# The out projection of a decoder layer: chunks 0 and 1 as a pair of seven half products, chunk 2 spread between them

## The chip, the core and the metric

The kernel runs on one core of a Trainium2 chip. The metric is the device time in microseconds (us), as the median of several runs; the trace beside it is one profiled execution. The engines are TensorE (PE: matmuls, with PEld for the weight loads ahead of them), VectorE (DVE), ScalarE (ACT), GpSimd (POOL) and SyncE (SP, which here only issues transfers). Each works through its own list of instructions in order; semaphores hold one engine until another has come to a point. A DMA can be issued by SP, ACT or POOL.

## The reference

One decoder layer on 256 positions of 2048 features, in float32. What matters here is its middle: the merged branches are multiplied by `w_out` and added to `x`, and the result goes to the FFN.

```
SEQ, D_MODEL, D_FF = 256, 2048, 5632
h = rms_norm(x, g_attn[l])
proj = h @ w_in[l]                       # queries, keys, values, forget gates, ga, gb
...
merged = sigmoid(ga) * (o_a @ w_br_fox[l]) + sigmoid(gb) * (o_b @ w_br_dil[l])
x = x + merged @ w_out[l]                # the out projection: 256 x 2048 by 2048 x 2048
h = rms_norm(x, g_ffn[l])
u = h @ w_up[l]                          # 2048 x 11264, then a causal convolution, SwiGLU
...
x = x + (silu(gate) * val) @ w_down[l]
```

## The kernel before

**Products and units.** A float32 product is made of three: each operand is split into a high part (what TensorE's fp32r type keeps) and a low part (the rest), and w_hi·a_h + w_lo·a_h + w_hi·a_l is summed in PSUM. The work is a list of *units*, one weight tile of 256 x 512 each (512 KB). A whole unit makes 12 matmuls of 128x512: 2 blocks of 128 rows x 2 slices of 128 features x 3 (`rows_unit`). The time of the kernel is that of TensorE's list of units, from unit 0 to the last.

**The way of a weight tile.** A DMA brings it into a buffer: `raw` has 4 slots (RAW_SLOTS), `raw_x` and `raw_y` have two each. Then ACT writes its high part into `w_hi` (`high(n)`, L1259), DVE subtracts and writes the low part into `w_lo` (`low(n)`, L1776), and TensorE reads both. `w_hi` and `w_lo` have 6 slots (RING): beside unit n, ACT and DVE make the parts of unit n+6, and `high` waits until unit n has been used. Three semaphores count units: `hi_done`, `lo_done`, `used`. SP reloads a `raw` slot when the low part of the unit that held it is done.

**Products of a pair.** The gates and the FFN, but in the kernel before not the out projection, have a second form. Two chunks of 512 columns are taken together, a matrix of 2 x 2 blocks on the features and columns, and half of the features go through seven products, P1 to P7, instead of eight (Strassen's scheme in Winograd's form). Such a product covers one block of 128 rows, as two half units q = 0, 1 of 6 matmuls each; the other features go through plain units. Its operands are sums: of the activations (`make_sums` and the parts P3, P5, P6, P7, made by DVE, split by ACT and DVE: `part_high`, `part_low`) and of the weight tiles. The sums of weights are made in place in `raw_x` and `raw_y`: by an *adding transfer* (POOL issues a DMA that adds the tile from memory to what the buffer holds), or by a sum on DVE (L1785, in `low`). Within a pair the order is P3, P1, P7, P6, P5, P2, P4. P1's tile is in raw_x, P3's in raw_y; P7 and P6 are in raw_y, P5 and P2 in raw_x, P4 in raw_y. P3's and P5's sums of weights come by adding transfer, P7's by DVE; for P6's follower P4 (the *fourth product* of raw_y) `low` has DVE add raw_x to raw_y at P2. The products land in PSUM banks that also collect plain units; copies on ACT (negated or not) and sums on DVE carry products from bank to bank.

**The branch stage**, ahead of the out projection, has 32 units in four chunks (BR_UNIT). After each chunk DVE adds the branch's banks to `work` (`dil_part`, L2120), then the two branches to `tmp` (L2124); TensorE turns `tmp` by transposes, ACT copies the high parts into `actA` (L1285, `merged_high`), DVE the low parts (L1828, `merged_low`). A chunk of `merged` is done once per branch chunk; the last one (chunk 3) in the out projection.

**The out projection** (OUT_UNIT, 24 units) has chunks 0, 1 and 2 of 512 columns, 8 units each, in this order. OUT_BANKS gives two banks to each, one per block of rows. At the end of a chunk `add_x2` on DVE adds both banks to `xr`, the copy of `x` in `work` (L2156), which ACT had loaded again with one DMA of 2 MB at unit 1 (x_again); TensorE then turns the sum (`turn_x2`), ACT copies it (`x2t_copy`) and sums its squares (`x2_squares`). Chunk 3 stands in block 0 of the FFN, as "O" units between its first products. Behind unit 3 of chunk 2 DVE makes the FFN's sums (`make_sums`, L1904 to L1909); ACT splits them at units 4 and 5, DVE at units 5 and 6. The loads of the FFN's first products are behind the last load of the out projection on SP's queue.

What sets the order around the change is written out by hand: each engine has its own loop over the same list of units, and what it does beside a unit is tied to the unit's place.

```
RING = 6
QU = 2
PAIRS = 7
OUT_BANKS = ((6, 7), (1, 3), (0, 2))
```

PAIRS is the number of pairs in the gates; the index PAIRS (the eighth) is free there.

## Time and profile before

| | us |
|---|---|
| median of 3 runs | 1336.09 (1335.77 to 1336.88) |
| the profiled execution | 1335.9 |
| its span, first to last instruction | 1333.9 |
| TensorE busy in it | 1329.0 |
| DVE busy | 1121.8 |
| ACT busy | 941.5 |
| out projection on TensorE, 552.90 to the FFN's first product at 621.04 | 68.1 |

The profiled execution takes 2.0 us more than its span, for what lies around the first and the last instruction. The page gives the busy time of each engine over the span, the chain of work that ended last, and the costliest groups of instructions. A row of the timeline has the start, the duration, the engine, the line, the operation and its tiles, and in brackets the idle time ahead of it with what ended that. Matmuls overlap: the duration of one is longer than the distance to the next, and only the distance adds up.

### The profile page before, as it was taken

What the parts mean: (1) busy time and instruction counts of PE and PEld (TensorE: products, weight loads), DVE (VectorE), ACT (ScalarE), POOL (GpSimd) and SP (SyncE); (2) the same over time, 40 slices, a digit from 0 to 9 for tenths busy, and PEclk for the clock granted to TensorE, in tenths of its full rate; (3) what the DMA queues carried; (4) which work ended last, traced back from release to release, by engine and by line L of the source; (5) the groups of instructions that cost most, each with busy time, mean ns of one, the idle gap of its engine ahead of it and who ended that gap; (6) DMA issues with size and microseconds to landing.
All of it is one profiled execution on the core that took longest, in us unless ns stands there. A gap on an engine that the chain in (4) does not pass through costs nothing.

```text
span 1333.9 us, 16454 instructions
## 1 busy us (share of the span) xinstructions
PE 1329.0 (100%) x6055; PEld 1101.7 (83%) x6055; DVE 1121.8 (84%) x1334; ACT 941.5 (71%) x1181; POOL 156.4 (12%) x175
## 2 busy tenths in 40 slices
PE   9999999999999999999999999999999999999999
PEld 7888888888888888888888888888888888888887
DVE  6868787888888876657688898999999999999996
ACT  6666666666666654446777778888888888888872
POOL 0121212021011000001010101111111102020200
PEclk9999999999999999999999999999999999999999
DMA  9877685758888654667879688999989899999952
GB/s 357 285 176 255 143 268 115 246 145 239 229 219 227 206 177 171 213 228 224 273 171 335 159 301 171 314 219 283 245 254 268 229 288 213 302 209 311 202 192 106
DMA packets 118191, 305.73 MB, mean 229 GB/s; under 512 B 11864, under 2 KB 13152, under 8 KB 117600
## 3 DMA queue, kind: packets, MB, share of 16 engines
q1 hardware_dynamic: 92304, 234.57, 50.5%
q0 software_dynamic: 21728, 66.07, 27.8%
q10 hardware_dynamic: 4080, 4.05, 0.9%
q8 instruction: 48, 0.79, 0.3%
q14 instruction: 31, 0.25, 0.1%
HBM read 302.55 MB, written 2.11 MB: 228 GB/s over the span
## 4 chain that ended last, share of the span: by engine, by line
PE 98%; DMA 1%; DVE 0%; ACT 0%; issue 0%; SPq 0%; ACTq 0%
PE acc L746 13%; PE acc L750 13%; PE acc L748 13%; PE acc L786 9%; PE acc L790 9%; PE acc L788 9%; PE acc L973 4%; PE acc L977 4%; PE acc L975 4%; PE acc L948 3%; PE acc L950 3%; PE acc L952 3%; PE acc L1085 1%; PE acc L769 1%; PE acc L767 1%; PE acc L771 1%
## 5 line engine op out<-in xcount | busy, mean ns | idle before, releaser
L1776 DVE TENSOR_TENSOR w_lo<-raw,w_hi 128x1024 fp32r<-128x1024 f32 x233 | 282.6, 1220 | 89.2 <-ACT w_hi L1259 87.9
L1259 ACT ACTIVATE w_hi<-raw 128x1024 fp32r<-128x1024 f32 x233 | 243.7, 1054 | 110.2 <-PE acc L750 76.6
L746 PE MATMUL acc<-w_hi,actA 128*128 128x512 f32 x660 | 259.7, 394 | 0.1
L750 PE MATMUL acc<-w_hi,actA 128*128 128x512 f32 x660 | 257.3, 390 | 0.0
L748 PE MATMUL acc<-w_lo,actA 128*128 128x512 f32 x660 | 256.9, 389 | 0.0
L1259 ACT ACTIVATE w_hi<-raw_y 128x1024 fp32r<-128x1024 f32 x144 | 149.8, 1058 | 75.4 <-PE acc L750 22.6
L1776 DVE TENSOR_TENSOR w_lo<-raw_y,w_hi 128x1024 fp32r<-128x1024 f32 x144 | 173.2, 1219 | 23.4 <-ACT w_hi L1259 22.1
L1776 DVE TENSOR_TENSOR w_lo<-raw_x,w_hi 128x1024 fp32r<-128x1024 f32 x108 | 129.9, 1219 | 40.5 <-ACT w_hi L1259 40.1
L750 PEld LDWEIGHTS acc<-w_hi,actA 128*128 128x128 f32 x660 | 123.9, 188 | 26.1
L746 PEld LDWEIGHTS acc<-w_hi,actA 128*128 128x128 f32 x660 | 123.9, 188 | 25.5 <-issue 0.7
L748 PEld LDWEIGHTS acc<-w_lo,actA 128*128 128x128 f32 x660 | 124.0, 188 | 24.9
L1259 ACT ACTIVATE w_hi<-raw_x 128x1024 fp32r<-128x1024 f32 x108 | 111.1, 1051 | 36.4 <-DMA raw_x<-w_in 19.3
L786 PE MATMUL acc<-w_hi,actB 128*128 128x512 f32 x296 | 116.3, 393 | 0.0
L790 PE MATMUL acc<-w_hi,actB 128*128 128x512 f32 x296 | 115.4, 390 | 0.0
L788 PE MATMUL acc<-w_lo,actB 128*128 128x512 f32 x296 | 115.1, 389 | 0.0
L973 PE MATMUL acc<-w_hi,actA 128*128 128x512 f32 x224 | 88.3, 394 | 0.0
L977 PE MATMUL acc<-w_hi,actA 128*128 128x512 f32 x224 | 87.3, 390 | 0.0
L975 PE MATMUL acc<-w_lo,actA 128*128 128x512 f32 x224 | 87.2, 389 | 0.0
L2422 POOL DMA_DIRECT2D raw_y<-w_up x34 | 29.5, 868 | 459.1 <-DVE w_lo L1776 458.9
L1259 ACT ACTIVATE w_hi<-odd 128x1024 fp32r<-128x1024 f32 x63 | 66.3, 1053 | 17.3 <-PE acc L790 9.9
L1776 DVE TENSOR_TENSOR w_lo<-odd,w_hi 128x1024 fp32r<-128x1024 f32 x63 | 76.7, 1217 | 1.8 <-ACT w_hi L1259 1.8
L2195 DVE SCALAR_TENSOR_TENSOR work<-acc,smalls_sb,work 128x255 f32<-128x255 f32 (+1 forms) x176 | 72.4, 473 | 3.4 <-ACT work L1595 3.3
(300 smaller groups left out, 2606.9 us busy)
## 6 DMA issues: line engine op xcount, KB each, us to landing
raw<-w_in SPq DMA_DIRECT2D x101, 512.0 KB, 4.7
raw<-w_down SPq DMA_DIRECT2D x59, 512.0 KB, 5.6
raw_x<-w_up SPq DMA_DIRECT2D x44, 512.0 KB, 5.0
raw_y<-w_up POOLq DMA_DIRECT2D x34, 512.0 KB, 7.4
raw_x<-w_in SPq DMA_DIRECT2D x28, 512.0 KB, 4.0
raw<-w_out SPq DMA_DIRECT2D x28, 512.0 KB, 4.6
odd<-w_up SPq DMA_DIRECT2D x27, 512.0 KB, 5.1
work<-w_up SPq DMA_DIRECT2D x24, 512.0 KB, 5.5
```

The costliest lines, as they stand in the source:

```text
L746: nc.tensor.matmul(o, lhsT=a_h, rhs=w_hi[:, s, k, :], start=first and k == 0, stop=False, skip_group_check=onto_seed)
L748: nc.tensor.matmul(o, lhsT=a_h, rhs=w_lo[:, s, k, :], start=False, stop=False, skip_group_check=onto_seed)
L750: mm = nc.tensor.matmul(o, lhsT=a_l, rhs=w_hi[:, s, k, :], start=False, stop=last and k == KU - 1, skip_group_check=onto_seed)
L786: nc.tensor.matmul(o, lhsT=a_h, rhs=w_hi[:, s, k, :], start=first and k == 0, stop=False, skip_group_check=True)
L788: nc.tensor.matmul(o, lhsT=a_h, rhs=w_lo[:, s, k, :], start=False, stop=False, skip_group_check=True)
L790: mm = nc.tensor.matmul(o, lhsT=a_l, rhs=w_hi[:, s, k, :], start=False, stop=last and k == KU - 1, skip_group_check=True)
L973: nc.tensor.matmul(o, lhsT=a_h, rhs=w_hi[:, s, k, :], start=side == 0 and j == 0 and k == 0, stop=False, skip_group_check=True)
L975: nc.tensor.matmul(o, lhsT=a_h, rhs=w_lo[:, s, k, :], start=False, stop=False, skip_group_check=True)
L977: mm = nc.tensor.matmul(o, lhsT=a_l, rhs=w_hi[:, s, k, :], start=False, stop=kt == KT - 1, skip_group_check=True)
L1259: nc.scalar.activation(w_hi[:, n % RING, :, :], src.rearrange("p (k n) -> p k n", k=KU), ACT.Copy).then_inc(hi_done, 1)
L1776: nc.vector.tensor_tensor(w_lo[:, n % RING, :, :], src.rearrange("p (k n) -> p k n", k=KU), w_hi[:, n % RING, :, :].bitcast(f32), ALU.subt ...
L2195: t = nc.vector.scalar_tensor_tensor(out=conv[:, j, lag:SEQ], in0=bank[(4, 7)[j // 2]][:, (j % 2) * SEQ:(j % 2 + 1) * SEQ - lag], scalar=s ...
```

## The change

**What it does.** Chunks 0 and 1 of the out projection become a pair (index PAIRS, 7, in the tables of the gates). Its first eight slices of features go through the seven products on half of the rows' blocks, 14 half units "H"; the other eight through plain units "G" (side 0 and 1, plain 0 to 3), 8 of them. Chunk 2's eight units "C" are spread: `out_units` writes the order C0, P3, C1, P1, C2, P7, P6, G00, P5, G01, G10, P2, G02, P4, G03, G11, G12, G13, C3 to C7, 30 units (each P is two half units; G01 is side 0 plain 1).

**Banks and sums.** OUT_BANKS now names a bank for each product; chunk 2 has banks 6 and 7. ACT copies P1 (negated) from bank 0 to bank 1, P7 from bank 3 to `tmp`, P6 (negated) from bank 0 to `tmp` (`out_sum`). DVE adds bank 0 to `xr` (g_u0) ahead of the second row block of G10, subtracts P7 and adds P6 (`out_bank_sums`). TensorE waits for g_v7 ahead of G00's second row block and for g_u0 ahead of G10's. `add_x2` is left for chunk 2 alone.

**Operands.** ACT makes a second, whole copy of the turned `merged` in `odd` (`merged_turned`); DVE subtracts there (`make_merged`, at the end of the branch stage), ACT and DVE split the results (`merged_part_high`, `merged_part_low`). ACT makes P1's negated parts with two copies.

**Loads.** 24 tiles become 28: SP loads 22, and POOL issues six adding transfers, two each for P3, P5 (as in the gates) and for P4. P4's are the second point of the change: instead of the sum on DVE at P2, the adding transfer is issued when P6's low part is done. The reload of `x` is split in two DMAs of 1 MB, at P1's first half and at P5's first half. The FFN's first loads follow P2 and P4.

**Moved.** The transposes of chunk 3 of `merged` go behind C1 (they were behind unit 2 of chunk 0), those of chunk 0 of the new x behind G12, of chunk 1 behind C3. `make_sums` goes from behind unit 3 of chunk 2 to behind unit 4, the copies P3 and P1 of `part_high` from 4 to 5, P7 and P6 from 5 to 6, `part_low` from 5 and 6 to 6 and 7. The FFN's first O unit waits for `x2_done` 3.

The core of the diff (line numbers behind @@ are of before and after):

```diff
@@ -50,18 +50,18 @@
 def uses_before(i, q):
-    return (PAIRS if q < QU else 0) + i - first_block(q)
+    return (PAIRS + 1 if q < QU else 0) + i - first_block(q)
...
@@ -108,7 +108,29 @@
-FF_UNIT = OUT_UNIT + 3 * UPR
+def out_units():
...
+    units = third(0) + product("P3") + third(1) + product("P1") + third(2) + product("P7") + product("P6")
+    units += plain(0, 0) + product("P5") + plain(0, 1) + plain(1, 0) + product("P2") + plain(0, 2)
+    return units + product("P4") + plain(0, 3) + plain(1, 1, 2, 3) + third(*range(3, UPR))
...
@@ -161,7 +196,7 @@
-OUT_BANKS = ((6, 7), (1, 3), (0, 2))
+OUT_BANKS = {"P3": 2, "P1": 0, "P7": 3, "P6": 0, "P5": 0, "P2": 1, "P4": 3}
@@ -671,16 +719,43 @@ SP
...
+            for n, unit in enumerate(OUTS, OUT_UNIT):
+                if unit[0] != "H":
+                    k = OUT_LOAD_AT[unit] + RAW_SLOTS
+                    if k < len(OUT_LOADS):
+                        sp.wait_ge(lo_done, n)
+                        load_out(k)
+                    continue
+                _, c, name, q = unit
+                if name == "P5":
+                    sp.wait_ge(lo_done, n)
+                    load_gate_b21(c, q)
+                elif name == "P2":
+                    sp.wait_ge(lo_done, n)
+                    load_b11(0, q)
...
@@ -1059,23 +1134,77 @@ TensorE
+            def out_product(n, name, q):
+                if q == 0:
+                    if name == "P3":
+                        pe.wait_ge(dil_merged, 4)
+                        pe.wait_ge(h_part_lo, 5)
+                    elif name == "P1":
+                        pe.wait_ge(h_part_hi, 9)
+                    elif name == "P7":
+                        pe.wait_ge(h_part_lo, 6)
+                    elif name == "P6":
+                        pe.wait_ge(h_part_lo, 7)
+                        pe.wait_ge(g_p1, PAIRS + 1)
+                    elif name == "P5":
+                        pe.wait_ge(h_part_lo, 8)
+                        pe.wait_ge(g_v, PAIRS + 1)
+                o = bank[OUT_BANKS[name]]
+                pe.wait_ge(lo_done, n)
...
+            def out_plain(n, side, j):
+                pe.wait_ge(mt_lo, 6 if j < 2 else 8)
+                pe.wait_ge(lo_done, n)
+                s = n % RING
+                for r, o in enumerate((bank[2], bank[0]) if side else (bank[1], bank[3])):
+                    if r and j == 0:
+                        pe.wait_ge(g_u0 if side else g_v7, PAIRS + 1)
...
@@ -1186,6 +1315,8 @@
                 if unit[0] == "O":
                     u = unit[2]
+                    if u == 0:
+                        pe.wait_ge(x2_done, 3)
@@ -1564,24 +1704,59 @@ ACT
+                    elif c == 3 and u == 1:
+                        act.wait_ge(mt_lo, 2)
+                        merged_part_high("P3", 12)
+                        for half in range(2):
+                            nc.scalar.activation(own[:, 0, :, half * P:half * P + P],
+                                                 gate_quarter(0, 0, half).bitcast(f32), ACT.Copy, scale=-1.0)\
+                                .then_inc(h_part_hi, 1)
...
+            def out_sum(n, name):
+                act.wait_ge(used, n + 1)
+                if name == "P1":
+                    act.wait_ge(dil_merged, 3)
+                    nc.scalar.activation(bank[1], bank[0], ACT.Copy, scale=-1.0).then_inc(g_p1, 1)
+                elif name == "P7":
+                    nc.scalar.activation(tmp[:, 1, :], bank[3], ACT.Copy).then_inc(g_v7, 1)
+                else:
+                    nc.scalar.activation(tmp[:, 0, :], bank[0], ACT.Copy, scale=-1.0).then_inc(g_v, 1)
...
+                elif unit == ("H", PAIRS, "P1", 0):
+                    act.dma_start(xr[:, :, 0:2 * NB], x_rows[:, :, 0:2 * NB]).then_inc(x_again, 16)
+                elif unit == ("H", PAIRS, "P5", 0):
+                    act.wait_ge(x_again, 16)
+                    act.dma_start(xr[:, :, 2 * NB:], x_rows[:, :, 2 * NB:]).then_inc(x_again, 16)
...
@@ -1775,12 +1951,12 @@ DVE, in low
-                if (GATE_UNIT <= n < BR_UNIT and GATES[n - GATE_UNIT][2] == "P2"
+                if (pair and name == "P2" and c < PAIRS
                         or n >= FF_UNIT and FFN[n - FF_UNIT][2] == "P2" and not fourth_by_transfer(i, q)):
...
@@ -2138,6 +2314,23 @@ DVE
+            def make_merged():
+                x11, x21, x12, x22 = (merged_sum[name] for name in ("P6", "P7", "P3", "P5"))
+                nc.vector.tensor_tensor(x22, x21, x22, ALU.subtract).then_inc(h_made, 1)
...
+            def merged_part_low(name, n_hi):
+                dve.wait_ge(h_part_hi, n_hi)
...
+                    elif c == 3 and u == 0:
+                        make_merged()
+                    elif c == 3 and u == 2:
+                        merged_part_low("P3", 7)
@@ -2156,23 +2353,59 @@
+            def out_bank_sums(n, unit):
+                if unit == ("H", PAIRS, "P5", QU - 1):
+                    dve.wait_ge(x_again, 16)
+                    dve.wait_ge(used, n + 1)
+                    add_bank(0, out_rows(0, 1)).then_inc(g_u0, 1)
+                elif unit == ("G", PAIRS, 0, 1):
+                    dve.wait_ge(g_v7, PAIRS + 1)
...
+                elif unit == ("C", 4):
+                    make_sums()
+                elif unit == ("C", 6):
+                    part_low("P3")
+                    part_low("P1")
...
@@ -2417,6 +2650,15 @@ POOL
+            third_sum(PAIRS, 0)
+            third_sum(PAIRS, 1)
+            first_sum(PAIRS, 0)
+            first_sum(PAIRS, 1)
+            for q in range(QU):
+                pool.wait_ge(lo_done, OUT_AT["H", PAIRS, "P6", q])
+                nc.gpsimd.dma_start(raw_y[:, q, :].rearrange("p (k n) -> p k n", k=KU),
+                                    w_out_v[:, KU * (QU + q):KU * (QU + q) + KU, 0:NB], accum_op=ALU.add)\
+                    .then_inc(y_summed[q], 16)
```

**Where instructions stand.** The three pieces below list DVE's and POOL's instructions in their order, before and after; the lines of after are its own (L1952 is `low`, L1776 before; L2360 `add_bank`; L2616 and L2659 adding transfers).

DVE from the low parts behind the last `merged_low` to chunk 1's sums, before (L2156 is `add_x2`):

```order
L1776 TENSOR_TENSOR w_lo<-raw,w_hi 128x1024 [waits hi_done] x5
L1828 TENSOR_TENSOR actA<-acc,actA 128x2x256 [waits mt_hi] x2
L1776 TENSOR_TENSOR w_lo<-raw,w_hi 128x1024 [waits hi_done] x3
L2156 TENSOR_TENSOR work<-acc,work 128x512 [waits unit_used,x_again]
L2156 TENSOR_TENSOR work<-acc,work 128x512
L1776 TENSOR_TENSOR w_lo<-raw,w_hi 128x1024 [waits hi_done] x8
L2156 TENSOR_TENSOR work<-acc,work 128x512 [waits unit_used]
L2156 TENSOR_TENSOR work<-acc,work 128x512
```

The same place after:

```order
L1952 TENSOR_TENSOR w_lo<-raw,w_hi 128x1024 [waits hi_done]
L1952 TENSOR_TENSOR w_lo<-raw_x,w_hi 128x1024 [waits hi_done] x2
L1952 TENSOR_TENSOR w_lo<-raw,w_hi 128x1024 [waits hi_done] x2
L1952 TENSOR_TENSOR w_lo<-raw_x,w_hi 128x1024 [waits hi_done] x2
L1952 TENSOR_TENSOR w_lo<-raw,w_hi 128x1024 [waits hi_done]
L2360 TENSOR_TENSOR work<-acc,work 128x512 [waits unit_used,x_again]
L1952 TENSOR_TENSOR w_lo<-raw_y,w_hi 128x1024 [waits hi_done]
L2370 TENSOR_TENSOR work<-work,tmp 128x512 [waits g_v7]
L1952 TENSOR_TENSOR w_lo<-raw_y,w_hi 128x1024 [waits hi_done]
L2374 TENSOR_TENSOR work<-work,tmp 128x512 [waits g_v]
```

The sum of bank 0 (L2360, g_u0) now stands behind the low parts of P2's two tiles (the second raw_x x2) and of G02 (raw), and the sums with P7 (L2370) and P6 (L2374) among P4's tiles; no sum of raw_y and raw_x stands at P2.

DVE at the end of the out projection, before (L1904 to L1909 `make_sums`, L1847 and L1844 low halves of FFN operands):

```order
L1776 TENSOR_TENSOR w_lo<-raw,w_hi 128x1024 [waits hi_done] x3
L1776 TENSOR_TENSOR w_lo<-raw_y,w_hi 128x1024 [waits hi_done] x2
L1904 TENSOR_TENSOR odd<-work 128x512 [waits x2t_done]
L1906 TENSOR_TENSOR odd<-work,odd 128x512 [waits part_made]
L1907 TENSOR_TENSOR odd<-work 128x512
L1909 TENSOR_TENSOR odd<-work,odd 128x512 [waits part_made]
L1776 TENSOR_TENSOR w_lo<-softmax,w_hi 128x1024 [waits hi_done]
L1776 TENSOR_TENSOR w_lo<-raw_x,w_hi 128x1024 [waits hi_done]
L1847 TENSOR_TENSOR actB<-odd,actB 128x4x128 [waits part_hi]
L1844 SCALAR_TENSOR_TENSOR actB<-work,actB 128x4x128 [waits part_hi]
L1776 TENSOR_TENSOR w_lo<-raw_x,w_hi 128x1024 [waits hi_done]
```

The same place after (L2080 to L2085 `make_sums`, L2023 and L2020 the low halves):

```order
L1952 TENSOR_TENSOR w_lo<-raw_y,w_hi 128x1024 [waits hi_done] x2
L1952 TENSOR_TENSOR w_lo<-softmax,w_hi 128x1024 [waits hi_done]
L2080 TENSOR_TENSOR odd<-work 128x512 [waits x2t_done]
L2082 TENSOR_TENSOR odd<-work,odd 128x512 [waits part_made]
L2083 TENSOR_TENSOR odd<-work 128x512
L2085 TENSOR_TENSOR odd<-work,odd 128x512 [waits part_made]
L1952 TENSOR_TENSOR w_lo<-raw_x,w_hi 128x1024 [waits hi_done] x2
L2023 TENSOR_TENSOR actB<-odd,actB 128x4x128 [waits part_hi]
L2020 SCALAR_TENSOR_TENSOR actB<-work,actB 128x4x128 [waits part_hi]
```

`make_sums` stands one tile later, behind the softmax buffer's tile (third of block 0's tiles made there) and not ahead of it, and the low halves behind both raw_x tiles and not between them.

POOL's adding transfers from the branch stage's end to the FFN's first, before:

```order
L2357 COPY st<-smalls_sb 128x1 [waits row_max]
L2359 TENSOR_TENSOR softmax<-consts_sb,st 128x384 [waits slope_now]
L2422 DMA raw_y<-w_up 128x1024 [waits lo_done] x2
L2422 DMA raw_x<-w_up 128x1024 [waits y_added0]
L2422 DMA raw_x<-w_up 128x1024 [waits y_added1]
L2422 DMA raw_y<-w_up 128x1024 [waits lo_done] x2
```

and after (w_out rows are new):

```order
L2590 COPY st<-smalls_sb 128x1 [waits row_max]
L2592 TENSOR_TENSOR softmax<-consts_sb,st 128x384 [waits slope_now]
L2616 DMA raw_y<-w_out 128x2x512 [waits lo_done] x2
L2616 DMA raw_x<-w_out 128x2x512 [waits y_added0]
L2616 DMA raw_x<-w_out 128x2x512 [waits y_added1]
L2659 DMA raw_y<-w_out 128x2x512 [waits lo_done] x2
L2664 DMA raw_y<-w_up 128x1024 [waits lo_done] x2
L2664 DMA raw_x<-w_up 128x1024 [waits y_added0]
L2664 DMA raw_x<-w_up 128x1024 [waits y_added1]
L2664 DMA raw_y<-w_up 128x1024 [waits lo_done] x2
```

The pair's six adding transfers stand ahead of the FFN's, the fourth product's two (L2659) last of the six.

## Rows read from the trace of the kernel before

**Rows 1.** Page, busy time; and windows: us, PE, PEld, DVE, ACT, POOL, PEclk, DMA, GB/s.

```profile
PE 1329.0 (100%) x6055; PEld 1101.7 (83%) x6055; DVE 1121.8 (84%) x1334; ACT 941.5 (71%) x1181; POOL 156.4 (12%) x175
...
552.00:618.00 66.00, 65.89 (x303) 54.49 (x302) 36.70 (x38) 32.46 (x45) 1.76 (x2) 1.00 0.76 257
```

**Rows 2.** Waits of TensorE: us in total, times, longest us.

```profile
PE acc L873 <- POOL actB L2371: 1.3, 1, 1.3
```

**Rows 3.** Timeline of TensorE at both ends of the out projection.

```profile
552.40 0.39 PE L750 MATMUL acc<-w_hi,actB 128*128 128x512 f32 x1
552.90 0.47 PE L746 MATMUL acc<-w_hi,actA 128*128 128x512 f32 x1
...
618.32 0.39 PE L746 MATMUL acc<-w_hi,actA 128*128 128x512 f32 x1
...
621.04 0.39 PE L786 MATMUL acc<-w_hi,actB 128*128 128x512 f32 x1
```

**Rows 4.** Timelines of DVE, then ACT, at the branch stage's end.

```profile
543.59 2.56 DVE L1776 TENSOR_TENSOR w_lo<-raw,w_hi 128x1024 fp32r<-128x1024 f32 x2
...
551.51 1.28 DVE L1828 TENSOR_TENSOR actA<-acc,actA 128x512 fp32r<-128x512 f32 x2
552.90 1.29 DVE L2120 TENSOR_TENSOR work<-acc,work 128x512 f32<-128x512 f32 x2
...
546.55 1.06 ACT L1259 ACTIVATE w_hi<-raw 128x1024 fp32r<-128x1024 f32 x1 [1.66 <-PE acc L750]
549.28 1.06 ACT L1259 ACTIVATE w_hi<-raw 128x1024 fp32r<-128x1024 f32 x1 [1.67 <-PE acc L750]
```

**Rows 5.** Timelines of ACT, then DVE, at the out projection's end.

```profile
610.42 1.06 ACT L1259 ACTIVATE w_hi<-raw_y 128x1024 fp32r<-128x1024 f32 x1 [1.12 <-PE acc L750]
...
615.43 0.64 ACT L1319 ACTIVATE actB<-odd 128x512 fp32r<-128x512 f32 x1 [1.23 <-DVE odd L1909]
615.97 0.62 ACT L1319 ACTIVATE actB<-work 128x512 fp32r<-128x512 f32 x1
...
611.51 1.23 DVE L1776 TENSOR_TENSOR w_lo<-raw_y,w_hi 128x1024 fp32r<-128x1024 f32 x1 [2.41 <-ACT w_hi L1259]
612.66 0.68 DVE L1904 TENSOR_TENSOR odd<-work 128x512 f32<-128x512 f32 x1
...
618.71 0.68 DVE L1847 TENSOR_TENSOR actB<-odd,actB 128x512 fp32r<-128x512 f32 x1
```

**Rows 6.** Last gate pair: timelines of POOL, ACT, SP's queue and TensorE.

```profile
424.98 1.20 POOL L2383 DMA_DIRECT2D raw_x<-w_in  x1 [2.30 <-DVE raw_y L1785]
...
430.66 1.06 ACT L1259 ACTIVATE w_hi<-raw_x 128x1024 fp32r<-128x1024 f32 x1 [0.71 <-DMA raw_x<-w_in]
...
436.86 1.06 ACT L1259 ACTIVATE w_hi<-raw_x 128x1024 fp32r<-128x1024 f32 x1 [0.18 <-DMA raw_x<-w_in]
...
429.68 3.70 SPq L588 DMA_DIRECT2D raw_x<-w_in  x2
...
442.37 0.39 PE L948 MATMUL acc<-w_hi,actA 128*128 128x512 f32 x1
```

**Rows 7.** Transfers issued in 556 to 574: KB each, median us to landing.

```profile
raw<-w_out SPq DMA_DIRECT2D x7, 512.0 KB, 6.3
work<-x ACTq DMA_DIRECT2D x1, 2048.0 KB, 11.3
```

**Rows 8.** Transfers issued in 571 to 594.

```profile
raw<-w_out SPq DMA_DIRECT2D x9, 512.0 KB, 4.2
```

**Rows 9.** Transfers issued in 628 to 652, block 0 of the FFN.

```profile
raw_y<-w_up POOLq DMA_DIRECT2D x2, 512.0 KB, 10.4
raw_x<-w_up SPq DMA_DIRECT2D x2, 512.0 KB, 8.6
```

**Rows 10.** Timeline of TensorE at the kernel's start.

```profile
1.32 4.21 PE L873 MATMUL acc<-actB 128*128 128x512 f32 x9 [1.32 <-POOL actB L2371]
5.32 0.54 PE L844 MATMUL acc<-w_hi,actA 128*128 128x512 f32 x1
```

261 lines of the change are left out of this document (190 added, 71 removed).

## The prediction

> **What bounds the kernel now.** Four views, in this order. The page's busy times first: TensorE is busy for 1329.0 of 1333.9 us [rows 1], so a product taken away counts in full unless something makes TensorE wait. Then its waits: the one of any size is the 1.3 us ahead of the first instruction [rows 2]. The out projection has the granted clock 1.00 (2.4 GHz) over the whole stretch [rows 1]. Then TensorE's timeline: a product of 128x512 starts every 0.227 us (the 0.39 us of a row is latency), so a unit of 12 takes 2.72 us, 618.32 to 621.04 [rows 3], and one of 6 products 1.36 us. Last, what the other engines have in hand over TensorE, because each weight tile passes load, ACT's high part and DVE's low part, in order on each engine: a late tile also holds whatever stands behind it on ACT and DVE. So the question is not how much work is removed, but which of these queues comes late.
>
> **Removed: 12 products.** Chunks 0 and 1 were 16 units of 12, 192 products. Now they are 14 half units of 6 (84) and 8 plain units of 12 (96), 180 together. 12 x 0.227 = 2.72 us, on the path in full. The three transposes of the stage stay, moved.
>
> **The first product, P3.** Before, the stage starts 0.50 us after the last branch product, 552.40 to 552.90, a wait of 0.27, for DVE's merged halves (551.51 + 1.28) [rows 3, 4]. Now chunk 2's first unit (C0) needs only older halves: it starts at 552.63 and ends at 555.35. P3 then waits for two things that the change itself makes late: its operand, and bank 2, which the last dil_part empties. DVE's two lows end at 546.15 [rows 4]; the four new subtractions take 2.75 us (the same four in block 0: 612.66 to about 615.4 [rows 5]), to 548.9. ACT, free at 547.6 after the tile of 546.55, waits for that and then makes three part copies, 0.54 apart, to 550.6; the tile that started at 549.28 is 1.3 us late, and so are the merged halves behind it. DVE adds P3's low half (0.6) ahead of them: halves 553.4 to 554.7, dil_part (1.29) to 556.0. P3 waits 0.65 us; less the 0.27 that goes: **+0.4 us** (0 if ACT's copies are quicker, 0.8 with one more late step).
>
> **The end of the stage.** In before the chain to block 0's P3 is: tile 610.42, low 611.51, four sums from 612.66, part copies on ACT from 615.43, another tile, its low, P3's low half 618.71 to 619.4 [rows 5]. P3 starts at 621.04 [rows 3], 1.65 us later. The change puts make_sums behind C4, the copies behind C5 and the low half behind C6, each one unit nearer to the end. 2.72 - 1.65 = **+1.1 us** (0.8 to 1.3). Nothing covers it: the same operations in the same order, all of them with rows. Block 0's unit O0 now waits for chunk 2's sums: DVE 0.1 + 1.29 after the stage, against 2.72 of P3's two halves, so nothing.
>
> **The transfers in the middle.** With P3 at 556.0, TensorE without waits goes on with P3, C1, eight transposes, P1 and C2: 4 x 2.72 + 0.95 (552.90 to 621.04 less 24 x 2.72 leaves 2.9 us for three such sets [rows 3]), P7 at 567.8. P7 and P6 lead to side 0 plain 0 at 573.3 (its second row block 1.36 later, 574.6), P5 at 576.0, and side 1 plain 0 at 581.4 (second row block at 582.8). Both second blocks have a new wait.
> First g_v7, an ACT copy of bank 3. DVE, behind dil_part, has the merged add (1.23), three lows (1.14 apart), a part (0.6) and P7's first sum (1.23): 556.0 + 6.5 = 562.5, and a low and a sum later, at 564.9, the second; GpSimd issues the adding transfers for P5 there. In the last gate pair such a transfer issued at 424.98 was in at 430.66, where ACT waited for it: 5.7 us [rows 6]. Here the second has 2.4 us after the first, and half of x (1 MB) starts on ACT's queue at about 565.9. While the whole x flowed, loads of w_out took 6.3 us in the median against 4.2 alone, and x itself 11.3 [rows 7, 8]. I take 9 us for the second transfer, 574; ACT's tile (1.0) and the copy (0.6) end at 575.6. **+1.0 us** (0 with 5.7, 2 with 10).
> Then g_u0. It is a sum on DVE, and ahead of it DVE has the lows of both P2 tiles and of side 0 plain 2. P2's tiles are loaded by SP into the buffers that P5 has just left, so they are issued after P5's lows: 571.5 and about 576.3 (574 + 1.06 + 1.14). GpSimd's queue then still has the two adding transfers of the fourth product (the new part; one DVE sum each, 1.23 us, goes). Between adding transfers in block 0, SP's raw_x loads took 8.6 us and GpSimd's 10.4 in the median [rows 9]; in the gate pair, with the queue empty by then, P2's second tile was read at 436.86 after SP's issue at 433.0 (the row of two issues ends at 433.38), some 3.9 us [rows 6]. With 3.9 the second tile is in at 580.2, and tile, two lows and the sum (1.06 + 1.14 + 1.14 + 0.7, some 4.1 us) end at 584.3, against 583.8 needed after the first wait: +0.5. With 8.6: 584.9, 589.0, +5.2. The nearer row is the one with 8.6, since adding transfers and SP's loads are under way together as there, though with fewer loads: I take 7.7, **+4.3 us**. For the range, 0 (if x and the sums come no later than in the gate pair) to 5.2.
> After that P2's lows are done, and the fourth product's transfers have 20 us.
> The Trainium skill, DMA: Bandwidth & Descriptors, section Issuing engines are not separate DMA queues, says that DMAs started by different engines run on the same 16 DMA engines and interleave. The trace agrees (6.3 against 4.2 us). With queues of their own the +1.0 and +4.3 would be gone, and the sum would be the first rival's.
>
> **Edits that cost nothing.** ACT gets 6 part copies, 4 copies of turned halves, 3 bank copies and 6 more tiles, about 15 us over 75; it is busy 32.5 of 66 us there [rows 1]. DVE gets 6 lows, 8 sums and parts, 2 P7 sums and 3 bank sums, some 17 us on 36.7 of 66 [rows 1]. Room is left in sum; the order costs, and that stands above. If this cover were gone, each further low would be 1.2 us. The loads for the first four tiles are issued in the branch stage, 20 us ahead. Loads grow from 24 tiles to 28, half a megabyte each.
>
> **Sum.** -2.72 + 0.4 + 1.1 + 1.0 + 4.3 = +4.1 us on the profiled execution's 1335.9 (span 1333.9 and 2.0 around it): 1340.0. The median of the runs is 0.2 above that execution; I say 1340.2.
>
> **Rivals.**
> 1. The transfers land in time, not slower: x in two halves of 4 KB rows disturbs less than 2 MB at once, and the gate pair runs the same pattern with no wait on TensorE. For it: there P2's first half started at 442.37, five us after its second tile was read at 436.86 [rows 6]. Against it: no x and no fourth transfer there, and no sum of DVE behind those lows. It decides at P2's second tile: in by 578.7 (4.1 ahead of 582.8), no wait. Sum -2.72 + 0.4 + 1.1 = -1.2: 1334.9.
> 2. The low halves are in time too, at both ends, and nothing waits: -2.72 - 0.27 = -3.0, 1333.1. Against it are the durations of rows 4 and 5, that do not depend on transfers.
> 3. It gets worse at the same place: the second P5 transfer takes 11 us as x did, so everything behind it moves 2 us on, and TensorE stands for 6 to 7 us there. If the clock falls in such a wait, that costs more: the nine products at the start took 4.0 us instead of 9 x 0.227 = 2.0 [rows 10], a loss of 2.0 us. Sum about +6.1 to +8.1: 1342.2 to 1344.2.
> The Trainium skill, TensorE: Matmul & The Clock Gate, section The HAM clock gate, says that an idle array goes back to 1.2 GHz, and that activity gives 2.4 back. No row of before shows it: TensorE never idles after its start. By that rule alone the forecast would be up to 2 us higher.
>
> **How the numbers follow.** The forecast 0.63, of which I put 0.17 where about half of the +4.3 is hidden, 1336.5 to 1338.7; rival 1 0.20, since the two transfer prices are the least certain terms; rival 2 0.06, rival 3 0.11. A measurement of this kernel can tell about 0.2% from no change, 2.7 us: slower begins at 1338.8, faster ends at 1333.4. Slower 0.46 + 0.11 = 0.57; same 0.17 + 0.20 = 0.37; faster 0.06. The range must take in rival 1, since without it and rival 2 more than 2 in 10 would be left out; it leaves out rival 2 and the upper half of rival 3: 1334.6 to 1343.3, that is, from just below rival 1 to just above the waits at their upper ends (-2.72 + 0.8 + 1.3 + 2 + 5.2 = +6.6, 1342.7).
>
> **What would show it.** Right: 12 products fewer; P3 of the stage some 0.6 us after C0, released by DVE; a gap of 3 to 5 us ahead of the second row block of side 1 plain 0, with DVE's row for g_u0 ending just before it and ACT's P2 tiles idle before a DMA; a gap of 1.1 us ahead of block 0's P3. Wrong: no gap above 1 us on TensorE between 560 and 590, and SP's raw_x loads of w_out landing in some 4 us; or a gap that starts at a step that I costed at nothing.

## The result and the profile after

| | before | after |
|---|---|---|
| median of the runs, us | 1336.18 (6 runs, 1335.77 to 1336.88) | 1342.13 (6 runs, 1341.08 to 1343.68) |
| ratio to before | | 1.0045, 95% interval 1.0033 to 1.0058 |
| the profiled execution, us | 1335.9 | 1341.08 |
| its span, us | 1333.9 | 1339.3 |

The kernel became 6.0 us slower. The time lies within the predicted range (1334.6 to 1343.3), 1.9 us above the predicted 1340.2, and almost exactly where the third rival began (1342.2).

The page of the kernel after, busy times (against [rows 1]), and the waits of TensorE (against [rows 2], where the only one of any size was the 1.3 us at the start; its line is left out here). `issue` in place of a releaser means that the profile names none:

```profile
PE 1328.7 (99%) x6043; PEld 1100.9 (82%) x6043; DVE 1137.9 (85%) x1353; ACT 952.9 (71%) x1200; POOL 163.4 (12%) x181
```

```profile
PE acc L1180 <- ACT tmp L1722: 3.0, 1, 3.0
...
PE acc L861 <- issue: 1.3, 1, 1.3
PE acc L1180 <- DVE work L2360: 1.3, 1, 1.3
PE acc L1160 <- DVE work L2296: 0.4, 1, 0.4
```

There are 12 products fewer (6055 to 6043), but four waits of 0.4 to 3.0 us that were not there: for P7's copy (ACT, L1722) ahead of side 0 plain 0's second row block, 3.0 us; for the sum of bank 0 (DVE, L2360, g_u0) ahead of side 1 plain 0's, 1.3; ahead of the FFN's first product 1.3; and for dil_part (L2296) ahead of P3, 0.4. The timeline of TensorE at these places (start, duration, engine, line; against [rows 3]):

```profile
554.86 0.39 PE L825 MATMUL acc<-w_hi,actA 128*128 128x512 f32 x1
555.69 0.50 PE L1160 MATMUL acc<-w_hi,actB 128*128 128x512 f32 x1 [0.45 <-DVE work L2296]
...
574.22 0.39 PE L1184 MATMUL acc<-w_hi,actA 128*128 128x512 f32 x1
577.62 0.50 PE L1180 MATMUL acc<-w_hi,actA 128*128 128x512 f32 x1 [3.01 <-ACT tmp L1722]
...
579.18 0.69 PE L1160 MATMUL acc<-w_hi,actB 128*128 128x512 f32 x1
579.67 0.63 PE L1162 MATMUL acc<-w_lo,actB 128*128 128x512 f32 x1
...
587.37 0.39 PE L1184 MATMUL acc<-w_hi,actA 128*128 128x512 f32 x1
589.02 0.50 PE L1180 MATMUL acc<-w_hi,actA 128*128 128x512 f32 x1 [1.26 <-DVE work L2360]
...
624.75 0.39 PE L825 MATMUL acc<-w_hi,actA 128*128 128x512 f32 x1
626.40 0.47 PE L861 MATMUL acc<-w_hi,actB 128*128 128x512 f32 x1 [1.27 <-issue]
```

From one start to the next a product has 0.227 us. What is above that was lost: 0.60 ahead of P3 (0.27 stood there before), 3.17 and 1.43 in the middle, 1.43 at the end. Behind the 3.0 us wait there is a fifth loss that is no wait: from 579.18 on products start 0.43 us apart, seven of them, which is 7 x 0.2 = 1.4 us. The windows view shows it as a lower granted clock (PEclk, 1.00 is 2.4 GHz; columns: us; busy us of PE, PEld, DVE, ACT, POOL with their counts; PEclk, DMA share, GB/s):

```profile
574.00:590.00 16.00, 11.72 (x43) 8.84 (x42) 8.90 (x8) 8.88 (x10) 0.00 (x0) 0.89 1.03 310
579.00:583.00 4.00, 4.00 (x12) 3.18 (x11) 2.00 (x2) 1.39 (x3) 0.00 (x0) 0.57 1.07 300
```

0.57 over these 4 us is a mix of the two levels, 1.2 and 2.4 GHz. The sum for this execution is -2.72 + 0.33 + 3.17 + 1.4 + 1.43 + 1.43 = +5.0 us; the two profiled executions differ by 1341.08 - 1335.9 = 5.2.

Where the 3.0 us come from is read on the other engines. POOL and the queues of SP and ACT issue transfers, ACT reads what has landed (against [rows 6]):

```profile
564.86 1.20 POOL L2616 DMA_DIRECT2D raw_x<-w_out  x1 [0.82 <-DVE raw_y L1961]
566.60 1.19 POOL L2659 DMA_DIRECT2D raw_y<-w_out  x1 [0.54 <-DVE w_lo L1952]
...
573.13 5.61 SPq L636 DMA_DIRECT2D raw_x<-w_out  x2
...
564.60 0.39 ACTq L1742 DMA_DIRECT2D work<-x  x1
...
576.03 1.06 ACT L1392 ACTIVATE w_hi<-raw_x 128x1024 fp32r<-128x1024 f32 x1 [4.19 <-DMA raw_x<-w_out]
576.99 0.58 ACT L1722 ACTIVATE tmp<-acc 128x512 f32<-128x512 f32 x1
...
582.56 1.06 ACT L1392 ACTIVATE w_hi<-raw_x 128x1024 fp32r<-128x1024 f32 x1 [2.61 <-DMA raw_x<-w_out]
584.91 1.06 ACT L1392 ACTIVATE w_hi<-raw_x 128x1024 fp32r<-128x1024 f32 x1 [1.29 <-DMA raw_x<-w_out]
```

P5's second adding transfer, issued at 564.86, is read at 576.03: 11.2 us, where the gate pair's took 5.7 [rows 6]. ACT stands for 4.19 us ahead of that tile, and the copy of P7 (576.99) is behind it. P2's two tiles, which SP's row of two loads brings, are read late as well (582.56 and 584.91). The transfers issued from 556 to 574 (KB each, median us to landing; against [rows 7]):

```profile
raw_x<-w_out POOLq DMA_DIRECT2D x2, 512.0 KB, 9.5
work<-x ACTq DMA_DIRECT2D x1, 1024.0 KB, 10.4
raw_y<-w_out POOLq DMA_DIRECT2D x2, 512.0 KB, 14.6
```

And DVE, where the sum of bank 0 (L2360) follows on the low part of G02:

```profile
587.15 1.22 DVE L1952 TENSOR_TENSOR w_lo<-raw,w_hi 128x1024 fp32r<-128x1024 f32 x1
588.28 0.68 DVE L2360 TENSOR_TENSOR work<-acc,work 128x512 f32<-128x512 f32 x1
```

The 1.3 us at the end stand behind this chain (against [rows 5]): squares of the new x on ACT, a tile and its low part, `make_sums`, P3's low half, which ends just ahead of 626.40:

```profile
616.10 0.65 ACT L1436 ACTIVATE odd<-work 128x512 f32<-128x512 f32 x1
...
617.33 1.07 ACT L1392 ACTIVATE w_hi<-softmax 128x1024 fp32r<-128x1024 f32 x1
...
619.79 1.06 ACT L1392 ACTIVATE w_hi<-raw_x 128x1024 fp32r<-128x1024 f32 x1 [1.40 <-PE acc L825]
...
619.57 0.68 DVE L2080 TENSOR_TENSOR odd<-work 128x512 f32<-128x512 f32 x1
...
625.62 0.68 DVE L2023 TENSOR_TENSOR actB<-odd,actB 128x512 fp32r<-128x512 f32 x1
```

### The profile page after: what moved, and what is told of

The parts are those of the page before. It is cut to its first block, busy times and chain, and to the rows that moved or that the text cites. A ratio compares the mean times of both kernels' runs of the same rounds, so it can differ in the third digit from the quotient of the medians.

```text
span 1339.3 us, 16497 instructions
## 1 busy us (share of the span) xinstructions
PE 1328.7 (99%) x6043; PEld 1100.9 (82%) x6043; DVE 1137.9 (85%) x1353; ACT 952.9 (71%) x1200; POOL 163.4 (12%) x181
## 4 chain that ended last, share of the span: by engine, by line
PE 95%; DVE 2%; DMA 2%; ACT 1%; issue 0%; POOL 0%; ACTq 0%; DVEq 0%; POOLq 0%
PE acc L821 12%; PE acc L825 12%; PE acc L823 12%; PE acc L861 9%; PE acc L865 9%; PE acc L863 9%; PE acc L1052 4%; PE acc L1048 4%; PE acc L1050 4%; PE acc L1027 3%; PE acc L1025 3%; PE acc L1023 3%; PE acc L1214 1%; DMA raw_x<-w_out 1%; PE acc L846 1%; PE acc L842 1%
## 5 line engine op out<-in xcount | busy, mean ns | idle before, releaser
L1952 DVE TENSOR_TENSOR w_lo<-raw,w_hi 128x1024 fp32r<-128x1024 f32 x225 | 272.8, 1221 | 67.6 <-ACT w_hi L1392 66.3
L1392 ACT ACTIVATE w_hi<-raw 128x1024 fp32r<-128x1024 f32 x225 | 235.2, 1054 | 85.1 <-PE acc L825 47.3
L821 PE MATMUL acc<-w_hi,actA 128*128 128x512 f32 x596 | 234.8, 394 | 0.0
L825 PE MATMUL acc<-w_hi,actA 128*128 128x512 f32 x596 | 232.6, 390 | 0.0
L823 PE MATMUL acc<-w_lo,actA 128*128 128x512 f32 x596 | 232.3, 390 | 0.0
L1392 ACT ACTIVATE w_hi<-raw_y 128x1024 fp32r<-128x1024 f32 x152 | 158.1, 1058 | 79.1 <-PE acc L825 23.3
L1952 DVE TENSOR_TENSOR w_lo<-raw_y,w_hi 128x1024 fp32r<-128x1024 f32 x152 | 183.1, 1220 | 20.5 <-ACT w_hi L1392 18.9
L1952 DVE TENSOR_TENSOR w_lo<-raw_x,w_hi 128x1024 fp32r<-128x1024 f32 x114 | 137.4, 1221 | 51.6 <-ACT w_hi L1392 51.3
L1392 ACT ACTIVATE w_hi<-raw_x 128x1024 fp32r<-128x1024 f32 x114 | 117.6, 1052 | 50.9 <-DMA raw_x<-w_in 21.6
L825 PEld LDWEIGHTS acc<-w_hi,actA 128*128 128x128 f32 x596 | 111.9, 188 | 23.5
L821 PEld LDWEIGHTS acc<-w_hi,actA 128*128 128x128 f32 x596 | 112.0, 188 | 22.5 <-issue 0.2
L823 PEld LDWEIGHTS acc<-w_lo,actA 128*128 128x128 f32 x596 | 112.1, 188 | 22.4
L1048 PE MATMUL acc<-w_hi,actA 128*128 128x512 f32 x224 | 88.4, 395 | 0.0
L1052 PE MATMUL acc<-w_hi,actA 128*128 128x512 f32 x224 | 87.4, 390 | 0.0
L1050 PE MATMUL acc<-w_lo,actA 128*128 128x512 f32 x224 | 87.3, 390 | 0.0
L1952 DVE TENSOR_TENSOR w_lo<-odd,w_hi 128x1024 fp32r<-128x1024 f32 x63 | 76.8, 1219 | 1.8 <-ACT w_hi L1392 1.8
```

What stands on the lines that cost most here:

```text
L821: nc.tensor.matmul(o, lhsT=a_h, rhs=w_hi[:, s, k, :], start=first and k == 0, stop=False, skip_group_check=onto_seed)
L823: nc.tensor.matmul(o, lhsT=a_h, rhs=w_lo[:, s, k, :], start=False, stop=False, skip_group_check=onto_seed)
L825: mm = nc.tensor.matmul(o, lhsT=a_l, rhs=w_hi[:, s, k, :], start=False, stop=last and k == KU - 1, skip_group_check=onto_seed)
L1048: nc.tensor.matmul(o, lhsT=a_h, rhs=w_hi[:, s, k, :], start=side == 0 and j == 0 and k == 0, stop=False, skip_group_check=True)
L1050: nc.tensor.matmul(o, lhsT=a_h, rhs=w_lo[:, s, k, :], start=False, stop=False, skip_group_check=True)
L1052: mm = nc.tensor.matmul(o, lhsT=a_l, rhs=w_hi[:, s, k, :], start=False, stop=kt == KT - 1, skip_group_check=True)
```

## The experiments

Three things could have stretched or held the middle: the reload of x, the fourth product's adding transfers, and the places of P7's copy and of the sum of bank 0 in their engines' orders. The first four kernels change one each, the later ones put the working parts together. Times are medians; each set of four ran on one chip beside the kernel before, which was at 1335.94, 1335.83 and 1336.03 us; the third set's chip was another than that of the first two. A trace shows one execution only. That of the kernel after, above, is the lowest of its six runs; in six of the kernels below (x's half alone, the sum alone, x's half with the fourth product, chunk 2's second unit, the fourth product on top of the end, the busy TensorE) it is the highest of theirs.

### x's first half earlier

```diff
-                elif unit == ("H", PAIRS, "P1", 0):
+                if unit == ("C", 0):
+                    act.wait_ge(merged, 4)
                     act.dma_start(xr[:, :, 0:2 * NB], x_rows[:, :, 0:2 * NB]).then_inc(x_again, 16)
...
```

> Edit: the first half of x is issued on ScalarE's queue about 8 us earlier, behind chunk 2's first unit (about 556.9), when the trace of after shows the DMA engines nearly idle (557 to 564). Theory X (x's half is what stretches the pair's second adding transfer from 5.7 to 11.2 us): it lands about 4 us earlier, the wait ahead of side 0 plain 0's second row block goes from 3.0 us to under 1, the clock does not fall, and the time drops by 3 to 5 us, to about 1337 to 1339. Theory F (the fourth product's two adding transfers, issued 1.7 and 3.5 us after it, stretch it): no change beyond 1 us, 1341 to 1343.

Measured 1340.56 us (1338.62 to 1341.66), ratio 1.0035 (1.0022 to 1.0047). The read of P5's second tile, and the waits and the window behind it:

```profile
565.35 1.20 POOL L2617 DMA_DIRECT2D raw_x<-w_out  x1 [0.82 <-DVE raw_y L1962]
...
573.19 1.06 ACT L1392 ACTIVATE w_hi<-raw_x 128x1024 fp32r<-128x1024 f32 x1 [1.37 <-DMA raw_x<-w_out]
```

```profile
PE acc L1180 <- DVE work L2361: 3.3, 1, 3.3
```

```profile
586.00:593.00 7.00, 6.40 (x16) 5.00 (x17) 5.24 (x6) 2.27 (x3) 0.00 (x0) 0.52 1.03 412
```

The transfer takes 7.8 us instead of 11.2, and the first wait is gone, as theory X said. But the time fell by 1.6 us only, not by 3 to 5 (the intervals of the two kernels against before overlap, so the size of this is rough): TensorE now comes earlier to the sum of bank 0 and waits 3.3 us there instead of 1.3, and the clock falls behind that wait (0.52 in this window). The cause of the first wait was x; the expected gain was given back one step later. So theory X held for the transfer and failed for the time.

### The fourth product's operand by VectorE

```diff
...
-                if (pair and name == "P2" and c < PAIRS
+                if (pair and name == "P2"
...
-                pool.wait_ge(lo_done, OUT_AT["H", PAIRS, "P6", q])
-                nc.gpsimd.dma_start(raw_y[:, q, :].rearrange("p (k n) -> p k n", k=KU),
-                                    w_out_v[:, KU * (QU + q):KU * (QU + q) + KU, 0:NB], accum_op=ALU.add)\
-                    .then_inc(y_summed[q], 16)
```

> Edit: the fourth product's operand is summed by VectorE at P2, as in the gates, and the two adding transfers are left out. Theory F: the pair's second adding transfer lands 3 us or more earlier, the wait ahead of side 0 plain 0's second row block falls below 1 us, and the time drops by 2 to 4 us, to 1338 to 1340, although VectorE has two sums of 1.23 us more. Theory X: the transfer takes 10 us or more as before; the two sums stand ahead of the sum of bank 0, so the wait ahead of side 1 plain 0's second row block grows from 1.3 to 2.5 to 3.7 us, and the time rises by 1 to 2.4 us, to 1343 to 1344.5.

Measured 1340.76 us (1340.24 to 1341.15), ratio 1.0036 (1.0024 to 1.0049). ACT's reads of P5's second and P2's second tile:

```profile
565.21 1.21 POOL L2614 DMA_DIRECT2D raw_x<-w_out  x1 [0.82 <-DVE raw_y L1959]
...
576.19 1.06 ACT L1390 ACTIVATE w_hi<-raw_x 128x1024 fp32r<-128x1024 f32 x1 [4.18 <-DMA raw_x<-w_out]
...
582.21 1.06 ACT L1390 ACTIVATE w_hi<-raw_x 128x1024 fp32r<-128x1024 f32 x1 [1.15 <-DMA raw_x<-w_out]
```

P5's transfer still takes 11.0 us (565.21 to 576.19), with x beside it as before: theory F is wrong for the first wait, 2.8 us of which remain. But P2's second tile is read 2.7 us earlier than in the kernel after (582.21 against 584.91), and the second wait is gone in spite of VectorE's two sums, which theory X had not expected. So the fourth product's adding transfers delay P2's tiles, and x delays P5's.

### The sum of bank 0 earlier

```diff
-                if unit == ("H", PAIRS, "P5", QU - 1):
+                if unit == ("H", PAIRS, "P6", QU - 1):
                     dve.wait_ge(x_again, 16)
-                    dve.wait_ge(used, n + 1)
+                    dve.wait_ge(used, OUT_AT["H", PAIRS, "P5", QU - 1] + 1)
```

> Edit: VectorE's sum of bank 0 (g_u0) moves ahead of the low parts of P2's tiles; the transfers stay. Theory O (the place of the sum behind P2's late tiles makes the second wait): the wait of 1.3 us ahead of side 1 plain 0's second row block goes, the first wait of 3.0 us and the slower matmuls behind it stay: -1.4 us, about 1340.7. Rival: the wait only moves on to P2's second half unit, whose low part ends at about 587.0 and which TensorE then wants at about 586: -0.4 us, 1341.7.

Measured 1339.88 us (1338.72 to 1341.5), ratio 1.0029 (1.0018 to 1.0041): 2.2 us less, more than the 1.4 expected; where the other 0.8 come from is not shown. The only wait left in the middle is the first:

```profile
PE acc L1180 <- ACT tmp L1722: 3.0, 1, 3.0
```

Theory O held: the second wait belonged to the sum's place, and P2's half units did not take it over.

### P7's copy earlier

```diff
-                if unit in (("H", PAIRS, "P1", QU - 1), ("H", PAIRS, "P7", QU - 1), ("H", PAIRS, "P6", QU - 1)):
+                if unit in (("H", PAIRS, "P1", QU - 1), ("H", PAIRS, "P6", QU - 1)):
                     out_sum(n, unit[2])
+                elif unit == ("H", PAIRS, "P7", 0):
+                    out_sum(n + 1, unit[2])
```

> Edit: ScalarE's copy of P7 moves ahead of the high part of P5's second tile; the transfers stay. Theory of the queue (the second wait takes over what the first gives up, since the sum of bank 0 still ends at about 589): the first wait goes, P5's second half unit waits some 1.2 us for its tile, side 1 plain 0's second row block 4 us; together about what it was; -1.4 us if the clock then does not fall (1340.7), 0 if it falls in the later wait (1342). Rival (the place of the copy alone costs the 3.0 us and the clock): -4.4 us, 1337.7.

Measured 1344.15 us (1343.27 to 1344.27), ratio 1.006 (1.0047 to 1.0072): 2.0 us more than the kernel after, outside both expectations. Its waits in the middle, and the clock behind each:

```profile
PE acc L1160 <- issue: 2.1, 1, 2.1
PE acc L1180 <- DVE work L2362: 2.0, 1, 2.0
```

```profile
579.00:583.00 4.00, 3.33 (x10) 2.70 (x11) 2.75 (x3) 1.51 (x3) 0.00 (x0) 0.72 1.10 261
...
590.00:595.00 5.00, 4.67 (x13) 3.69 (x14) 4.87 (x6) 1.18 (x2) 0.00 (x0) 0.66 1.02 406
```

The first wait is gone from its place, and one of 2.1 us stands ahead of P5's second half unit and one of 2.0 for the sum of bank 0. So moving the copy alone gains nothing, as the theory of the queue said, though it had the two waits at 1.2 and 4 us. What it missed is the clock: it falls behind both waits (0.72 and 0.66).

### x's half and the sum together

Both edits above, x's and the sum's.

> Edit: x's first half early and VectorE's sum of bank 0 ahead of P2's lows, together. Theory Q (x stretched the second adding transfer, and the sum's place behind P2's tiles kept what was left of it): neither of the two waits in the middle is there, and the clock stays at 1.00; 3.2 + 1.4 + 1.4 = 6.0 us less than the changed kernel, about 1336.1 (1335.5 to 1337). Rival (the fourth product's transfers still hold P2's own tiles): TensorE would want P2's first half unit at 584.5 and the second at 585.9, their low parts were ready about 583.5 and 584.8 with x early, so 1 us in hand; if they come 2 us later a wait of 1 us is left, 1337 to 1338.

Measured 1336.04 us (1335.26 to 1336.86), ratio 1.0001 (0.9992 to 1.001), on the number of theory Q. In the trace TensorE has no wait between 557 and 618, and the clock is at 1.00:

```profile
581.15 1.06 ACT L1392 ACTIVATE w_hi<-raw_x 128x1024 fp32r<-128x1024 f32 x1 [4.03 <-DMA raw_x<-w_out]
582.51 1.06 ACT L1392 ACTIVATE w_hi<-raw_x 128x1024 fp32r<-128x1024 f32 x1 [0.29 <-DMA raw_x<-w_out]
```

```profile
574.00:590.00 16.00, 16.00 (x72) 13.24 (x71) 11.99 (x12) 10.94 (x13) 0.00 (x0) 1.00 1.04 337
```

Two edits that were worth 1.6 and 2.2 us alone are worth 6.1 together. The fourth product's transfers are still there and P2's tiles still late (581.15 and 582.51); nothing stands behind them that TensorE needs at once.

### x's half earlier, and the fourth product by VectorE

Both edits above, x's and the fourth product's.

> Edit: x's first half early, and the fourth product's operand summed by VectorE. Theory Q: P5's second transfer takes some 8 us and P2's loads under 5, but the two sums of 1.23 us and the low parts stand ahead of the sum of bank 0, which ends at about 585.3 where TensorE wants it at 583.2: one wait of 2 us, 1337 to 1339. Rival F (what is left after x is the two adding transfers alone): no wait in the middle, 1336.

Measured 1337.99 us (1337.38 to 1339.99), ratio 1.0017 (1.0008 to 1.0026), as theory Q said:

```profile
PE acc L1180 <- DVE work L2359: 2.0, 1, 2.0
```

With both sets of transfers out of the way the sum of bank 0 is still 2.0 us late, now behind VectorE's own two sums (1.2 us each) and P2's lows. So with those two sums its place behind P2's lows still costs a wait; what the place would cost without them this kernel does not show. The trace has the clock at 0.76 from 586 to 593, behind this wait, and is 2.0 us above the median.

### The end one unit earlier

```diff
-                elif unit == ("C", 4):
+                elif unit == ("C", 3):
                     make_sums()
-                elif unit == ("C", 6):
+                elif unit == ("C", 5):
                     part_low("P3")
                     part_low("P1")
-                elif unit == ("C", UPR - 1):
+                elif unit == ("C", 6):
                     part_low("P7")
```

and `part_high` on ACT behind units 4 and 5 instead of 5 and 6, on top of x's half and the sum.

> Edit: as the kernel with x and the sum moved, and make_sums, part_high and part_low one unit earlier (behind chunk 2's units 3, 4 and 5, 5 and 6). If the gap ahead of the FFN's first product comes from their place alone, it goes from 1.65 to 0.23 us, and the time is 1.4 us less than with x and the sum moved: about 1334.7. Rival (another operand of that product, its bank or its weight tile, comes last just behind): less than 0.5 us.

Measured 1333.95 us (1333.55 to 1335.29), ratio 0.9986 (0.9977 to 0.9995): 2.1 us less than with x and the sum alone, 0.7 more than expected (the two traced executions, 1334.06 and 1335.39, are 1.3 apart). All waits of TensorE but the one at the start:

```profile
PE acc L1160 <- DVE work L2297: 0.4, 1, 0.4
PE acc L874 <- DVE work L2361: 0.3, 1, 0.3
```

The wait ahead of the FFN's first product is gone; the place of its sums was the cause. All 11 runs of this kernel (up to 1335.29) are below all 33 of the kernel before beside it (from 1335.4).

### Further steps from there

Chunk 2's second unit and its transposes ahead of P3:

```diff
-    units = third(0) + product("P3") + third(1) + product("P1") + third(2) + product("P7") + product("P6")
+    units = third(0, 1) + product("P3") + product("P1") + third(2) + product("P7") + product("P6")
```

> Edit: as the kernel with x, the sum and the end moved, and chunk 2's second unit with its transposes ahead of P3 (the other engines' orders keep their places by position). P3's bank and operand then have 2.7 us more: the wait of 0.45 us ahead of it goes (0.6 us between the two matmuls), about 1334.1. Rival (P3's wait was cover for what follows, or P7's sums come later by the moved low parts): no change, 1334.7.

Measured 1333.52 us (1332.8 to 1336.08), ratio 0.9984 (0.9976 to 0.9993). The wait ahead of P3 is gone from the trace; the gain of 0.4 us against the kernel without it is within what the runs of both spread. The trace shows 1.7 us for chunk 0's sums ahead of its transposes; in the next kernel those transposes stand one unit later.

> Edit: as the kernel with x, the sum, the end and the start moved (1333.52), with chunk 0's transposes of the new x, its squares and its copy one unit later (behind side 1 plain 3). In that kernel's trace they wait 1.7 us for VectorE's sums, in the one without the moved start 0.3 us. If that wait comes in most executions, 0.3 to 1.5 us less: 1332 to 1333.2. Rival (only that execution had it): the same within 0.3 us, 1333.5; or the copy now comes late for the FFN's parts: slower.

Measured 1334.45 us (1333.46 to 1335.07), ratio 0.9987 (0.9978 to 0.9996). Here the 1.7 us are gone and the next transposes wait for ACT (0.8 us), so the rival is the nearer: no gain. These three kernels can't be told apart.

The fourth product's operand by VectorE, on top of x, the sum and the end:

> Edit: as the kernel with x, the sum and the end moved (1333.95), but the fourth product's operand summed by VectorE at P2 and not by adding transfers. Theory Q: with nothing of the middle late, the way of that sum decides nothing, since the lows of P2 come earlier without the two transfers and VectorE's two sums stand behind them: 1333.5 to 1334.4. Rival (the adding transfer is worth its two sums of 1.23 us, or part of them): 1334.9 to 1336.5.

Measured 1334.46 us (1333.95 to 1335.28), ratio 0.999 (0.9981 to 0.9999): between the two expectations, 0.5 us above the same kernel with the transfers (0.3 if each is set against the kernel before on its own chip) and within the spread. Once nothing waits, the adding transfer is worth at most about that.

### The price of the clock

```diff
+                    if r and j == 0 and side:
+                        pe.wait_ge(mt_hi, 8)
+                        for _ in range(13):
+                            nc.tensor.matmul(bank[4], lhsT=actA[:, 2 * HK, 0:P], rhs=w_hi[:, s, 0, :], start=True,
+                                             stop=True)
                     if r and j == 0:
                         pe.wait_ge(g_u0 if side else g_v7, PAIRS + 1)
```

on top of x's first half alone (1340.56).

> Edit: as the kernel with only x's first half early (1340.56; one wait of 3.3 us ahead of side 1 plain 0's second row block, and 13 of the products after it 0.2 us slower each), with 13 more products of 128x512 into a free bank (their result is not used) ahead of that wait. They need 13 x 0.227 = 2.95 us of it. Theory C (the idle TensorE is what lowers its clock afterwards, and that costs 2.6 us): no slower products behind the wait, and 2.0 to 2.6 us less, about 1338.2. Rival (the clock falls for another reason, or only the wait itself costs): no gain, 1340 to 1341.

Measured 1338.92 us (1337.56 to 1339.97), ratio 1.0022 (1.0013 to 1.0031). The window that had 0.52 with x's half alone:

```profile
586.00:593.00 7.00, 6.66 (x30) 5.15 (x29) 7.00 (x8) 4.41 (x5) 0.00 (x0) 1.00 1.00 400
```

The kernel does 13 products more and is 1.6 us faster (1.7 if each is set against the kernel before on its own chip). The clock is at 1.00, so the idle TensorE is what lowered it; over the whole execution it is 1.0 in all 11 runs here, and 0.997 to 0.999 in four of the five with x's half alone. The gain is under the 2.0 to 2.6 expected, most likely because the trace that they were read from was that kernel's highest run (1341.66).

### The kernel after, once more

> The changed kernel itself, beside the three others on the same chip: 1341 to 1343.7, as in its first runs.

Measured 1342.16 us (1341.41 to 1343.78), ratio 1.005 (1.0037 to 1.0063). This time the profiled execution took 1343.16 us, and it shows where its runs differ:

```profile
PE acc L1180 <- ACT tmp L1722: 3.2, 1, 3.2
PE acc L1180 <- DVE work L2360: 2.9, 1, 2.9
```

```profile
579.00:583.00 4.00, 4.00 (x19) 3.12 (x18) 2.39 (x2) 1.40 (x3) 0.00 (x0) 1.00 1.09 293
...
590.00:595.00 5.00, 5.00 (x17) 3.98 (x16) 4.05 (x5) 1.96 (x2) 0.00 (x0) 0.66 1.02 406
```

The first wait is the same (3.2 us), but the clock does not fall behind it (1.00). So from its restart on TensorE comes 1.6 us sooner to the sum of bank 0, which is no sooner, and waits 2.9 us instead of 1.3; the clock falls behind this second wait (0.66), where nothing takes the loss up. In the trace of 1341.08 us the fall came between the two waits, and the second one was shorter by as much. That is 2.1 us between two executions of one kernel; of its 11 runs four lie at 1341.1 to 1341.4, two at 1342.0 to 1342.2 and five at 1342.9 to 1343.8.

## Why the prediction was right, and where it was off

**The direction and the mechanism held.** 2.72 us were removed and paid for almost three times over by waits that the change itself makes. All four stand at places that the prediction named. Three have the releasers it named; for the fourth the profile names none, and TensorE goes on 0.1 us behind the end of P3's low half (626.30). One sign did not come: the gap of 3 to 5 us was forecast ahead of side 1 plain 0's second row block, and 1.3 and 2.9 us stood there in the two traces; the larger gap was ahead of side 0's.

**P3: +0.33, predicted +0.4.** TensorE continued at 555.69 behind dil_part, as worked out (556.0). Moving chunk 2's second unit ahead of it removed the wait.

**The end: +1.43, predicted +1.1 (0.8 to 1.3).** The step "the same operations in the same order" was wrong by a little: ACT now has the squares of chunk 1's new x (616.10 to 617.3) ahead of the tile at 617.33, on which the low part and `make_sums` follow; they stood elsewhere before. The next tile, which waits for TensorE, starts at 619.79, so by the step of one unit this one could have started 2.72 earlier, at 617.07: an estimate of 0.26 us for the squares. That they are the missing 0.3 us is read from the rows and was not tried by itself. That the place of the chain is the cause of the wait was: one unit earlier, it is gone.

**The middle: 6.0 us in the trace of 1341.08 and 7.9 in that of 1343.16, predicted 5.3, and divided differently.** The mis-sized term is the second adding transfer: I took 9 us between 5.7 and 10, and it took 11.2, as long as the 2 MB of x had [rows 7]. The row for x was named under rival 3 and not used as the upper end; it should have been: 1 MB of x beside it was enough (11.0 us also without the fourth product's transfers, 7.8 without x). So the first wait was 3.17 and not 1.0. P2's second load was issued 2.1 us later than taken (578.4 against 576.3) and took 1.2 us less (6.5 up to 584.91, against 7.7), so the sum of bank 0 ended only 0.9 us late, at 589.0 against 588.1. That these two errors partly cancel is luck. Since TensorE had lost more time earlier, by the wait and by the slower products, it lost less there: 1.43 instead of 4.3. Two waits in a row for one late chain do not add; the last one sets the sum.

**The clock, left to rival 3.** Its fall costs 1.4 to 1.6 us in these two traces, and whether this adds depends on its place: ahead of the second wait that wait takes it up, behind it it is lost. The prediction gave rival 3 (the transfer takes 11 us, TensorE stands 6 to 7 us, the clock falls, 1342.2 to 1344.2) a chance of 0.11. Its transfer came in both traces (11.2 and 11.3 us). All of it came in the trace of 1343.16, where TensorE waits 3.2 + 2.9 us and the clock falls; five of the kernel's 11 runs lie in rival 3's span. In the lowest four the time was about a microsecond above the forecast. Since x itself had taken 11.3 us [rows 7], rival 3 deserved more, and that the median still lies in the range is in part luck. The section The HAM clock gate of the Trainium skill's page TensorE: Matmul & The Clock Gate says that an idle array goes back to 1.2 GHz and that activity gives 2.4 back. The traces agree (0.57 behind the wait of 3.0 us, 0.52 behind 3.3, and 1.00 with the array kept busy), though a wait of 3.2 us once had no fall behind it.

**Rivals 1 and 2** are excluded for the change as it was made: P2's second tile was read at 584.9 and not by 578.7. But with x's half and one sum moved, TensorE has no wait in the middle, and the time is 1336.04, within 1.2 us of rival 1's 1334.9; that trace has three waits of 0.2 to 0.5 us at the kernel's start. So the gain of 12 products is there and was hidden by order and traffic, not by more work: that DVE and ACT have room, which was costed at nothing, held.

**The second part of the change**, the fourth product's operand, cost 1.4 us as it stands (1340.76 without it) by delaying P2's tiles, and at most gains 0.5 us where nothing waits.
